# Second-kind layers of a two-model chain: the forgetting softmax right behind its scores, both GELU halves together, no identity products ahead of the keys' transposition

## The reference

```python
h = rms_norm_2(x, norm_g)
z = h @ w_in                        # 1024 -> 3612 columns, split
# forgetting attention: 4 heads of 64
c = cumsum(log_sigmoid(ff + fox_b))
s = q @ k.T * 64**-0.5 + c[query] - c[key]
o_a = masked_softmax(s, causal) @ v * silu(f_gate)
# convolution: glu, 31 taps per channel, layer norm, silu, 256x256
o_b = conformer_conv(glu_in, ...) * silu(c_gate)
# sparse attention: 8 heads in 2 groups
hid = gelu((blocks(x_kc or x_vc) + pe) @ w1)   # compression, k and v
k_cmp, v_cmp = rope(hid_k @ k_w2), hid_v @ v_w2
o_cmp = masked_softmax(q @ k_cmp.T) @ v_cmp
o_slc, o_win = causal attention on selected and on window keys
o_c = (g0 * o_cmp + g1 * o_slc + g2 * o_win) * silu(n_gate)
x = x + concat(o_a, o_b, o_c) @ w_out
```

## Time and profile before

| | |
|---|---|
| median of 3 runs | 1655.81 us (1654.43 to 1656.41) |
| the profiled execution's own time | 1656.32 us |
| its span, first to last instruction | 1654.5 us |
| TensorE busy | 1609.5 us (97%) |
| VectorE busy | 1067.0 us (64%) |
| ScalarE busy | 825.9 us (50%) |
| GpSimd busy | 259.5 us (16%) |
| mean granted TensorE clock | 0.997 of full speed |

### The profile page before, as it was taken

The page is one execution under the profiler, slowest core; times in us unless marked ns, Lnnn a source line. Parts: engine busy times, 40 slices in busy tenths (PEclk is TensorE's granted clock), DMA queues, the critical chain, the costliest instruction groups (busy, mean ns, idle before and its releaser), DMA issues.

```text
span 1654.5 us, 27196 instructions
## 1 busy us (share of the span) xinstructions
PE 1609.5 (97%) x11196; PEld 1453.5 (88%) x11196; DVE 1067.0 (64%) x1269; ACT 825.9 (50%) x1123; POOL 259.5 (16%) x208
## 2 busy tenths in 40 slices
PE   7999999999999999999999999999999999999997
PEld 7999878888989999899988888898999898879885
DVE  4655557665755555655565767576555589968995
ACT  5443446653454343543454665345343465656563
POOL 0000060010000000000025001000000059405940
PEclk9999999999999999999999999999999999999999
DMA  7657555343455655466745434354656465146602
GB/s 227 224 181 232 173 177 173 124 130 96 161 177 180 201 178 195 158 198 191 232 160 174 160 110 148 105 182 149 206 183 196 133 213 195 33 135 205 203 33 89
DMA packets 206612, 273.97 MB, mean 166 GB/s; under 512 B 18774, under 2 KB 167096, under 8 KB 206008
## 3 DMA queue, kind: packets, MB, share of 16 engines
q1 hardware_dynamic: 206376, 272.67, 51.4%
q10 hardware_dynamic: 144, 0.00, 0.0%
HBM read 271.61 MB, written 1.08 MB: 165 GB/s over the span
## 4 chain that ended last, share of the span: by engine, by line
PE 86%; DVE 9%; ACT 2%; issue 1%; POOL 1%; DMA 0%; SPq 0%; POOLq 0%; ACTq 0%; DVEq 0%
PE bank L503 29%; PE bank L550 14%; PE bank L985 8%; PE bank L974 7%; PE bank L2037 5%; PE bank L1175 4%; DVE wlo L435 3%; PE bank L2293 2%; PE bank L1257 2%; PE bank L2015 2%; PE bank L1118 1%; PE bank L2190 1%; PE bank L1093 1%; DVE hT_lo L354 1%; ACT whi L424 1%
## 5 line engine op out<-in xcount | busy, mean ns | idle before, releaser
L435 DVE TENSOR_TENSOR wlo<-raw,whi 128x2048 fp32r<-128x2048 f32 (+2 forms) x258 | 583.3, 2264 | 331.4 <-ACT whi L424 330.7
L424 ACT ACTIVATE whi<-raw 128x2048 fp32r<-128x2048 f32 (+2 forms) x258 | 484.3, 1880 | 309.4 <-PE bank L550 101.4
L503 PE MATMUL bank<-hT_hi,whi 128*128 128x256 f32 x1408 | 395.1, 281 | 1.2 <-DVE wlo L435 0.4
L503 PE MATMUL bank<-hT_lo,whi 128*128 128x256 f32 x1408 | 393.3, 279 | 0.0
L503 PE MATMUL bank<-hT_hi,wlo 128*128 128x256 f32 x1408 | 393.2, 279 | 0.0
L503 PEld LDWEIGHTS bank<-hT_hi,whi 128*128 128x128 f32 x1408 | 265.3, 188 | 4.5 <-DVE wlo L435 1.4
L503 PEld LDWEIGHTS bank<-hT_lo,whi 128*128 128x128 f32 x1408 | 265.5, 189 | 1.4
L503 PEld LDWEIGHTS bank<-hT_hi,wlo 128*128 128x128 f32 x1408 | 265.4, 188 | 0.0
L550 PE MATMUL bank<-whi,Y 128*128 128x512 f32 x704 | 224.0, 390 | 0.0
L308 POOL TENSOR_TENSOR st<-st 128x1 f32<-128x1 f32 x18 | 17.6, 980 | 937.6 <-ACT X L301 937.6
L550 PEld LDWEIGHTS bank<-whi,Y 128*128 128x128 f32 x704 | 132.2, 188 | 26.8
(11 more groups left out here) (398 smaller groups left out, 2838.1 us busy)
## 6 DMA issues: line engine op xcount, KB each, us to landing
raw<-in_ffn_w SPq DMA_DIRECT2D x132, 1024.0 KB, 5.6
raw<-in_w_in SPq DMA_DIRECT2D x80, 1024.0 KB, 5.5
raw<-in_w_out SPq DMA_DIRECT2D x16, 1024.0 KB, 5.0
raw<-in_w_br_na SPq DMA_DIRECT2D x4, 1024.0 KB, 5.4
raw<-in_w_br_mla SPq DMA_DIRECT2D x4, 1024.0 KB, 5.1
raw<-in_w_br_gla SPq DMA_DIRECT2D x4, 1024.0 KB, 5.0
raw<-in_cmp_k_w SPq DMA_DIRECT2D x4, 1024.0 KB, 6.1
raw<-in_cmp_v_w SPq DMA_DIRECT2D x4, 1024.0 KB, 5.2
```

The lines of the kernel that those rows point to most:

```text
L424: act.activation(m["whi"][:, slot, 0:w], m["raw"][:, slot, 0:w], ACT.Copy).then_inc(s.hi_ready, 1)
L435: dve.tensor_tensor(m["wlo"][:, slot, 0:w], m["raw"][:, slot, 0:w], m["whi"][:, slot, 0:w].bitcast(F32), ALU.subtract).then_inc(s.lo_ready, 1)
L503: mm = pe.matmul(B[bank][:, mt * T:(mt + 1) * T], a, b, start=(n == 0 and k == 0), stop=(n == KK - 1 and k == 2))
```

## The change

The order of ScalarE's and VectorE's steps is altered in every second-kind layer, and the call that issues six identity products goes. TensorE's list stays.

```diff
 ACT2 = words("""
-    ... hi.8 tall.1-2 hi.9-12 exp.0 fv
-    hi.13-14 exp.1 hi.15-16 exp.2 tok_b.1 gelu.0 tok_b.0 turn.0 gelu.1 turn.1 ...
+    ... hi.8 tall.1-2 hi.9-10 exp.0-2
+    hi.11-12 fv hi.13-16 tok_b.1 gelu.0 tok_b.0 turn.0 gelu.1 turn.1 ...
 DVE2 = words("""
-    taps.0 lo.9 taps.1 peak.0 taps.2-3 lo.10-12 taps.4-5 sg lo.13 peak.1 taps.6 lo.14 peak.2 taps.7 lo.15 gelu.0 prob.0 gelu_out.0
-    gelu.1 lo.16 gelu_out.1 rotate cmp_kv ...
+    taps.0 lo.9 peak.0-2 taps.1-2 lo.10 prob.0 lo.11-12 taps.3-4 sg lo.13 taps.5 lo.14 taps.6-7 lo.15 gelu.0-1 gelu_out.0
+    lo.16 gelu_out.1 rotate cmp_kv ...
@@ def cmp_score():
-            idle_products(6)
             pe.wait_ge(s.kcmp_ready, past.kcmp_ready + 1)
             pe.transpose(B[6][:, 128:192], kc2, ident[0:64, 0:64]).then_inc(s.kcmpT_done, 1)
             idle_products(4)
```

More of the change, by code:

```diff
@@ L1856 @@
 ACT2 = words("""
-    sq.1 hh.0-15 hi.2 params hi.3 sm hi.4 decay hi.5 fox_own tall.4 hi.6 tall.0 hi.7 blk.0-1 hi.8 tall.1-2 hi.9-12 exp.0 fv
-    hi.13-14 exp.1 hi.15-16 exp.2 tok_b.1 gelu.0 tok_b.0 turn.0 gelu.1 turn.1 tall.5 hid_turn turn.2 hi.17 heads_turn hi.18
+    sq.1 hh.0-15 hi.2 params hi.3 sm hi.4 decay hi.5 fox_own tall.4 hi.6 tall.0 hi.7 blk.0-1 hi.8 tall.1-2 hi.9-10 exp.0-2
+    hi.11-12 fv hi.13-16 tok_b.1 gelu.0 tok_b.0 turn.0 gelu.1 turn.1 tall.5 hid_turn turn.2 hi.17 heads_turn hi.18
     cmp_prob exp.3-5 tall.6 cmp_turn exp.6-8 hi.19 tall.7 turn.3 exp.9 turn.4 exp.10 turn.5 exp.11 out.0 hi.20 turn.6 hi.21
@@ L1864 @@
     hl.0-1 scale.1 hl.2-14 lo.1 hl.15 lo.2-3 sm lo.4 decay fox_bias lo.5 tall.4 lo.6 tall.0 blk.0-1 blk_low.0 lo.7 blk_low.1 lo.8
-    taps.0 lo.9 taps.1 peak.0 taps.2-3 lo.10-12 taps.4-5 sg lo.13 peak.1 taps.6 lo.14 peak.2 taps.7 lo.15 gelu.0 prob.0 gelu_out.0
-    gelu.1 lo.16 gelu_out.1 rotate cmp_kv tall.5 cmp_score lo.17 cmp_shift peak.3 taps.8-9 peak.4-5 cmp_prob tall.6 prob.1
+    taps.0 lo.9 peak.0-2 taps.1-2 lo.10 prob.0 lo.11-12 taps.3-4 sg lo.13 taps.5 lo.14 taps.6-7 lo.15 gelu.0-1 gelu_out.0
+    lo.16 gelu_out.1 rotate cmp_kv tall.5 cmp_score lo.17 cmp_shift peak.3 taps.8-9 peak.4-5 cmp_prob tall.6 prob.1
     peak.6-8 taps.10-11 lo.18 prob.2 taps.12 peak.9 taps.13 peak.10 taps.14 peak.11 taps.15 out.0 prob.3 tall.7 peak.12
```

## The result

The changed kernel is slower: a median of 1661.11 us (1657.97 to 1663.19, 8 runs) against 1655.63 (1654.06 to 1656.41, 8 runs), a ratio of 1.0031 with a 95% interval of 1.0022 to 1.0040. The forecast was 1652.6, with a range up to 1656.1. The profiled execution took 1661.34 us, its span 1659.2, 4.7 more than before.

What follows compares the result with a forecast made beforehand. TensorE, busy for 97% of the span, was taken as the bound, with VectorE making it wait. Keys 1.60 us earlier in each of two layers gave 3.2 us, so 1655.8 - 3.2 = 1652.6 us, range 1650.3 to 1656.1.

Steps and rivals of the forecast that it cites:

- the first turn: TensorE's first turn in each second-kind layer: would no longer wait for the forgetting probabilities and start 1.36 us earlier.
- the keys: Compressed keys that VectorE hands to TensorE in each second-kind layer: forecast ready 1.60 us earlier, at 1407.0.
- the balance: VectorE's idle time ahead of the compressed keys, per layer: old gaps of 2.99 us go, 1.39 come, so 1.60 us earlier.
- the bounds that I gave: Gain per layer as VectorE's operations collide with GpSimd's taps: 2.3 us if kindly, 0.9 if one or two more collide.
- All behind moves by 1.60: Chain behind the compressed keys (gate, copies, compressed scores): claimed to keep the whole 1.60 us gain in each layer.
- The predicted 3.2 us: Whole gain forecast for the two second-kind layers: 2 x 1.60 us.
- TensorE stands bare from 1405.61 to 1407.0: TensorE ahead of turning the compressed keys, without identity products: 1.4 us idle; dropping the products alone worth 0.1 us.
- B: Rival: clock falls in both layers for twice 3 us, losing 6.0 us against 3.2 won: 1658.6 us; chance 0.05.
- A: Rival: clock falls behind the bare stretch, 3 us at half speed costing up to 1.5 per layer: 1655.6; chance 0.24.
- the stretch of 1442 to 1452: Layer norm in the earlier trace: transpositions, small products and 1.37 us idle kept clock 1.00; cited against a clock fall.
- both falls in the trace: Clock falls in the earlier trace, said to end by themselves after about 3 us; cited against a longer fall.

## Why the prediction was wrong, point by point

**Right: the first turn.** It was to start 1.36 us earlier and starts 1.33 earlier (37.84 to 36.51 from the first compression product), with no wait for line 2620. No weight split was late either: from 1330 to 1480 TensorE's waits show none for line 434 or 435.

**Mis-sized: the keys.** Forecast 1.60 us earlier, measured 1.10. The idle time of VectorE went as the balance said, from 2.99 to 1.33. But its busy time up to the keys grew by 0.56:

```profile
1373.84 5.23 DVE L435 TENSOR_TENSOR wlo<-raw,whi 128x2048 fp32r<-128x2048 f32 x2
...
1381.87 2.87 DVE L435 TENSOR_TENSOR wlo<-raw,whi 128x2048 fp32r<-128x2048 f32 x1
```

The split of unit 13 took 2.87 us where it had 2.29. It is the largest of several: the split of unit 14 took 2.71 (2.29 before), while prob.0 came down from 2.57 to 2.28 and the split of unit 15 from 2.45 to 2.29. This was inside the bounds that I gave (0.9 to 2.3), and GpSimd's narrow taps show whose it is: with them the splits of units 13, 14 and 15 take 2.29 each.

**Missed: a gain given back.** "All behind moves by 1.60" didn't hold to the end of the layer. With six products, of 1.1 us at the keys 0.8 and 0.6 arrived at w_out, because TensorE then waits for VectorE's gate at the layer norm's first product; with tall.7 earlier that wait went. The predicted 3.2 us would have been 1.4 had the clock held.

**The step that failed: "TensorE stands bare from 1405.61 to 1407.0".** I priced the bare stretch at nothing, and called the products worth 0.1 us by what their time covers. The stretch was 1.8 us and not 1.4, because the keys came 0.5 us later than forecast, and the clock fell behind it in both layers. What that costs is the difference of the changed kernel to the new order with six products: 2.73 and 2.83 us at w_out, 5.3 in the medians.

The mechanism was among the rivals. B had it: a fall in both layers that lasts for about twice the 3 us, 1658.6 us, slower as soon as a layer spends more than 3.2 us at half speed on TensorE's work. The falls lasted 6.8 us each. I gave A and B 0.29 together, for two reasons that didn't bear the weight. One was the stretch of 1442 to 1452, which kept its clock with a wait of 1.37 us: one case, and shorter than the wait that came. The other was that both falls in the trace ended after about 3 us (3.4 each). B's own reason for a longer fall, that nothing dense runs behind the keys, is not shown either: in the kernel with three products the clock fell at the start of both second-kind layers, with the same code behind it, for 6.8 us in the first and 3.4 in the second. And the 1.50 us of identity products in the earlier trace rows were an open sign: undressed, the wait of 1.68 us is as long as the 1.66 us ahead of the fall in the earlier trace rows.

**Open.** With the bare stretch at 1.5 us one of two layers fell, at 1.8 both, at 1.13 neither, and at 0.56 or less none of those profiled. The length alone doesn't decide, though. At the start of every second-kind layer TensorE stands for 1.66 us behind eight transpositions (1.67 in a few), in all 13 kernels profiled here, and the clock fell behind 8 of these 26 waits. The kernel before and the one with three products, same code, first second-kind layer:

```profile
1318.30 0.36 PE L2063 MATMUL bank<-whi,hT_hi 128*128 128x256 f32 x1 [1.66 <-DVE hT_lo L354]
1319.00:1325.00 6.00, 5.55 (x43) 4.96 (x42) 4.27 (x16) 5.01 (x14) 0.96 (x2) 1.00 0.02 4
...
1317.10 0.36 PE L2063 MATMUL bank<-whi,hT_hi 128*128 128x256 f32 x1 [1.66 <-DVE hT_lo L354]
1319.00:1325.00 6.00, 6.00 (x29) 5.47 (x28) 4.23 (x12) 5.03 (x14) 1.77 (x4) 0.50 0.12 20
```

What else decides whether a wait is followed by a fall, and for how long, no run here tells. So a bare wait of this length carries a cost that comes with some chance; the sum of the forecast had it at nothing. The changed kernel has also 0.3 us more outside its span than before (2.1 against 1.8), as have the kernels with the new order where taps.1 stands behind the peaks; no run tells why.

## What to carry to other kernels

Work without a reader isn't free to remove: ask first how long the engine stands once it is gone, and what follows. Where the wait can be shortened by filling another engine's gap, do that first. Here, with one step of taps moved, the new order without products is 4.0 to 4.9 us faster than the kernel before; dropping them from the old order gave a median 1.6 slower, with an interval that just reaches no change. A gain read at one wait is to be followed to the end of the stage, since a part of it can be lost at the next.

## What the hardware showed that I had not expected

- The clock did not fall in the wait but 2.4 us after it (1408.75 to 1411.1), when TensorE had been working again; in the second layer 1.9 us after it (1576.45 to 1578.35), and in the old order without products 1.5 (1574.96 to 1576.5). It held 0.50 for 6.8 us in these three against 3.4 us around the window of the earlier trace rows.
- Twelve float32 transpositions of the identity, 1.47 us of them, kept the clock at 1.00 behind the keys as well as six products did.
- The mean granted clock tracks the time from run to run: over all kernels timed here, 0.001 of it goes with 1.0 us of span within a kernel. Much of the spread between executions of one kernel is the clock.
- GpSimd's taps cost the kernel before about 5 us in all: with one column each, a single execution took 1650.96 us against a median of 1656.2.
